# A decoder layer in split float32: the start addresses of the staged operands of the down projection and of the turned rows of the output projections

## The reference, cut to what matters

```python
h = rmsnorm(x, norm_attn_g);  proj = h @ w_in
mix = concat(differential_attention(...), stick_breaking_attention(...))
x = x + mix @ w_out                                              # 1024 x 1024
h2 = rmsnorm(x, norm_ffn_g)
x = x + (silu(h2 @ w_gate) * (h2 @ w_up)) @ w_down               # 1024 x 2816, 2816 x 1024
return rmsnorm(x, final_norm_g)
```

## Time and profile before

| | us |
|---|---|
| median of 3 runs (lowest, highest) | 2987.25 (2986.71, 2993.16) |
| profiled execution, its own time | 2989.48 |
| its span, first to last instruction | 2987.5 |
| PE busy | 2893.5 (97% of the span) |
| PEld busy | 2596.9 (87%) |
| DVE busy | 1961.6 (66%) |
| ACT busy | 1585.1 (53%) |
| mean granted TensorE clock | 0.994 of full |

### The profile page before, as it was taken

One profiled execution on the slowest core, in us unless ns is written; L12 is line 12 of the kernel. 1 busy time (PEld: TensorE's weight loads), 2 busy tenths in 40 slices (PEclk: granted clock), 3 DMA queues, 4 the chain that ended last, 5 costly groups with the idle time before them and its releaser, 6 DMA issues.

```text
span 2987.5 us, 51857 instructions
## 1 busy us (share of the span) xinstructions
PE 2893.5 (97%) x19000; PEld 2596.9 (87%) x19000; DVE 1961.6 (66%) x2944; ACT 1585.1 (53%) x2672; POOL 913.2 (31%) x1022
## 2 busy tenths in 40 slices
PE   7999999899999999999999999999999999999998
PEld 6888778677777999999889998998889998999886
DVE  6215520276776777778668787876658878888656
ACT  5122211267777878887555555554445555645444
POOL 1922221156665877777301222111000000001100
PEclk9999999999999999999999999999999999999999
DMA  5488896446642440411339998999747775799964
GB/s 202 127 213 210 200 244 155 127 103 145 162 112 60 112 99 16 114 32 62 113 124 285 321 310 261 286 278 310 211 134 218 237 238 184 218 325 295 293 195 159
DMA packets 303482, 559.47 MB, mean 187 GB/s; under 512 B 32289, under 2 KB 70305, under 8 KB 302113
## 3 DMA queue, kind: packets, MB, share of 16 engines
q1 hardware_dynamic: 262912, 463.12, 49.0%
q0 software_dynamic: 39072, 92.30, 16.2%
q10 hardware_dynamic: 1312, 1.64, 0.2%
HBM read 449.98 MB, written 197.13 MB: 217 GB/s over the span
## 4 chain that ended last, share of the span: by engine, by line
PE 59%; DVE 9%; POOL 6%; ACT 3%; issue 2%; DMA 2%; SPq 0%; DVEq 0%; ACTq 0%; POOLq 0%
PE f_ps L2431 26%; PE f_ps L2323 18%; PE h_o L998 6%; PE h_t L984 3%; PE h_z L720 2%; PE h_z L723 2%; POOL h_more L1282 2%; POOL h_work L1282 2%; DVE h_negmax L1118 2%; DVE h_more L1234 2%; DVE h_more L1150 1%; DMA f_wraw<-sums_scratch 1%; ACT h_work L1017 1%; ACT h_more L1017 1%; POOL h_srstd L1327 1%
## 5 line engine op out<-in xcount | busy, mean ns | idle before, releaser
L1810 ACT ACTIVATE f_whi<-f_wraw 128x512 fp32r<-128x512 f32 x834 | 520.4, 626 | 409.5 <-PE f_ps L2431 269.3
L1817 DVE TENSOR_TENSOR f_wlo<-f_wraw,f_whi 128x512 fp32r<-128x512 f32 x834 | 574.8, 690 | 237.9 <-ACT f_whi L1810 234.9
L2431 PE MATMUL f_ps<-f_hi_s,f_whi 128*128 128x256 f32 x1408 | 394.3, 280 | 6.1 <-DVE f_up L2164 6.0
L2431 PE MATMUL f_ps<-f_hi_s,f_wlo 128*128 128x256 f32 x1408 | 393.5, 279 | 0.0
L2431 PE MATMUL f_ps<-f_lo_s,f_whi 128*128 128x256 f32 x1408 | 392.5, 279 | 0.0
L1322 POOL TENSOR_TENSOR h_work<-h_work,h_more 128x1024 f32<-128x1024 f32 (+3 forms) x192 | 302.2, 1586 | 110.3 <-DVE h_more L1234 97.5
L2431 PE MATMUL f_ps<-f_hi_a,f_whi 128*128 128x256 f32 x1056 | 296.7, 281 | 0.9 <-DVE f_second L2164 0.9
L2431 PE MATMUL f_ps<-f_lo_a,f_whi 128*128 128x256 f32 x1056 | 296.6, 281 | 0.0
L2431 PE MATMUL f_ps<-f_hi_a,f_wlo 128*128 128x256 f32 x1056 | 295.5, 280 | 0.0
L2431 PEld LDWEIGHTS f_ps<-f_hi_s,f_whi 128*128 128x128 f32 x1408 | 265.1, 188 | 7.5 <-DVE f_wlo L1817 4.1
L2431 PEld LDWEIGHTS f_ps<-f_lo_s,f_whi 128*128 128x128 f32 x1408 | 264.7, 188 | 0.0
(11 more groups left out here) (199 smaller groups left out, 6857.1 us busy)
## 6 DMA issues: line engine op xcount, KB each, us to landing
f_wraw<-in_w_stream SPq DMA_DIRECT2D x394, 256.0 KB, 4.1
f_wraw<-sums_scratch SPq DMA_DIRECT2D x352, 256.0 KB, 4.5
sums_scratch<-in_w_stream POOLq DMA_DIRECT2D x132, 256.0 KB, 5.2
act_scratch<-f_act SPq DMA_DIRECT2D x88, 256.0 KB, 3.9
combined_acts<-f_act SPq DMA_DIRECT2D x88, 256.0 KB, 5.1
f_wraw<-down_sums SPq DMA_DIRECT2D x88, 256.0 KB, 2.7
f_piece<-combined_acts SPq DMA_DIRECT2D x88, 256.0 KB, 2.9
down_sums<-in_w_stream POOLq DMA_DIRECT2D x66, 256.0 KB, 6.5
```

The lines of the kernel that those rows point to most:

```text
L1810: act.activation(w_hi[ring][:], w_raw[ring][:], ACT.Copy).then_inc(S["hi_split"], 1)
L1817: dve.tensor_tensor(w_lo[ring][:], w_raw[ring][:], w_hi[ring][:].bitcast(F32), ALU.subtract).then_inc(S["lo_split"], 1)
L2431: mm = pe.matmul(outs[i], w[ring][:, col], a[name][:, c, :], start=(c == 0 and m == 0), stop=(c == 3 and m == 2))
```

## The change

`STAGE_SHIFT` places the three stages 96, 256 and 448 bytes behind a multiple of 512, hi and lo alike; turned pair 0 goes 128 bytes and pair 1 320 bytes behind it. The weights stay where they are. The buffers behind the stages (`pieces` and all that follow up to `junk`) move up by 512 bytes to make room. No instruction is added, removed or moved on any engine, and no size, wait or count changes.

```diff
+STAGE_SHIFT = (96, 256, 448)
...
-    pieces = stage + STAGES * row
+    pieces = stage + STAGES * row + LINE
...
-    assert junk + half <= H["base"] and stage + 2 * 4 * KC * BLK <= others
+    assert junk + half <= H["base"] and stage + 2 * 4 * KC * BLK + 320 <= others
...
-    F["turned_hi"] = [at(f"thi{n}", [P, KC, BLK], home, F32R) for n, home in enumerate((operands, stage))]
-    F["turned_lo"] = [at(f"tlo{n}", [P, KC, BLK], home + 4 * KC * BLK, F32R) for n, home in enumerate((operands, stage))]
+    F["turned_hi"] = [at(f"thi{n}", [P, KC, BLK], home, F32R) for n, home in enumerate((operands + 128, stage + 320))]
+    F["turned_lo"] = [at(f"tlo{n}", [P, KC, BLK], home + 4 * KC * BLK, F32R) for n, home in enumerate((operands + 128, stage + 320))]
...
-    F["stage_hi"] = [at(f"shi{s}", [P, BLK], stage + row * s, F32R) for s in range(STAGES)]
-    F["stage_lo"] = [at(f"slo{s}", [P, BLK], stage + row * s + half, F32R) for s in range(STAGES)]
+    F["stage_hi"] = [at(f"shi{s}", [P, BLK], stage + row * s + STAGE_SHIFT[s], F32R) for s in range(STAGES)]
+    F["stage_lo"] = [at(f"slo{s}", [P, BLK], stage + row * s + half + STAGE_SHIFT[s], F32R) for s in range(STAGES)]
```

## The result

| | before | after |
|---|---|---|
| median of 20 runs each, us | 2987.06 | 2995.47 |
| ratio, 95% interval | | 1.0027 (1.0016 to 1.0038) |
| profiled execution, its own time, us | 2989.48 | 2990.06 |
| its span, us | 2987.5 | 2988.0 |
| PE busy, us | 2893.5 | 2907.2 |

The change made the kernel slower by 0.27%, some 8 us. I had forecast 2981 us. The two profiled executions hide this, with spans 0.5 us apart: the attention in front of the changed part ended 10 us earlier in the one of after, and that differs from run to run. The first matmul of project and the end of the span tell more.

What follows compares the result with a forecast made beforehand. TensorE's own matmul pace was taken as the bound, PE busy 97%. Savings of 3.5 + 0.7 + 2.6 = 6.8 us, 0.9 on the path, gave 6.1 us: 2987.25 to 2981.1 us, range 2968 to 2992.

Steps and rivals of the forecast that it cites:

- the six that save 1.9 ns: Gate part, 256 columns: distances 32, 64, 128, 256, 288, 416 each save about 1.9 ns a matmul against 120 at 0.
- Stages: Down, 1848 matmuls at distances 416, 256 and 64: 1.9 ns saved on each, 3.5 us.
- Turned pair 0: Project blocks 0 and 3, 384 matmuls at distance 384: 1.9 ns saved on each, taken from neighbours 288 and 416, 0.7 us.
- Turned pair 1: Project blocks 1 and 2, 384 matmuls at distance 192: 6.7 ns saved on each, 2.6 us.
- 0.9 on the path: Project and down: 0.9 of TensorE's matmul time stands on the path; the rest is lost to waits on DVE or DMA.
- The two groups of three products: Gate tile: products at 32, 64, 128 took 117.8 ns a matmul, those at 256, 288, 416 took 118.3.
- The one on the bank: Gate part: s3 alone goes to the fourth bank of its four, which could cause its 113.3 ns instead of distance 192.
- Slower: All 2616 project and down matmuls: shifted weights meet the stream at a costlier moment, 8.5 us more, 2995.7 us; chance 0.14.
- What spoke for it: Attention scores: two 512 column matmuls at distance 0 took 230 ns each, so more than 13.4 ns can be lost.
- what spoke against it: Gate tile, 256 columns: neither half averages above the 120 ns of distance 0.
- No change: Project and down: the 13.4 ns are a fixed weight-change cost or the reads don't touch; 2987 us, chance 0.23.
- a large gain: Project and down: every distance does what 192 does in the gate part, 15.7 us less, 2971.5 us; chance 0.18.

Runs made afterwards that it cites:

- run with halves: Changed kernel with each project and down matmul, except the last two units, cut into two of 256 columns with own weight loads; 3001.29 us (before: 2984.41).
- sweep: Changed kernel with stages shifted by 32, 64, 160, turned pairs by 192, 224, gate operands by 192 to 512; 3005.19 us (before: 2985.87).
- 192 throughout: Kernel before with all seven gate operands 192 bytes behind a multiple of 512, nothing else changed; ratio 0.9964.

## Why the prediction was wrong

What I had asked about is there: the pace depends on the distance between the stationary slice and the moving operand. That it is the two reads which disturb each other fits this, but it is an inference; no run takes the weight load away. The step that failed is "distances 416, 256 and 64 are among the six that save 1.9 ns", with its like for pair 0 and pair 1: prices read at 256 columns were carried to 512.

- **Stages, -3.5 us forecast.** Measured: 624 matmuls at 234.0, 612 at 227.6 and 612 at 229.1 ns for 226.7, together 6.6 us more.
- **Turned pair 0, -0.7 us forecast.** 384 at 232.9 (233.4 in block 0, 232.4 in block 3): 2.4 us more.
- **Turned pair 1, -2.6 us forecast,** the largest single gain by matmul. 384 at 233.4: 2.6 us more. At 512 columns 192 is among the slow ones.
- **Sum.** 11.6 us more on TensorE, of which 0.9 on the path is 10.4 us; the median shows 8.4, the back part 10.9. From first matmul to first matmul the projects took 4.4 us more for 5.0 on TensorE, and the down stages from (0, 3) on 4.7 for 5.2, so the share of 0.9 was right there. That 10.9 is so near to 10.4 is in part luck: 3.4 of it come from down (0, 0 to 2), which differs by as much between runs with one and the same down part, and gates 1 and 3 gave 1.5 back.
- **The reading behind the prices.** The two groups of three products that I took for six distances at one price mix what differs. Distance 256 is among them, which by itself takes 120 (seven operands at 0) and saves nothing; 64, which had 117.5 there, had 113.4 in the run with halves. So "six of seven distances save 1.9" was no property of the distances even at 256 columns.
- **The doubts.** I had named two. The one on the bank was void (sweep, and 192 throughout). The other, that the load is as long as the matmul at 256 columns and covers half of it at 512, was the one that counted, and I priced it only on the side of a gain. The run with halves shows that the width decides. How the width turns the order round, no run shows; it stays open.
- **The rule of the Trainium skill,** in "TensorE: Matmul & The Clock Gate", section "Step-by-step: what each phase is for", that the next weight load takes no read bandwidth from the running matmul, is not borne out by the traces. By it no distance would matter, but the paces move by up to 7.3 ns of 226.7 and by 6.7 of 120.0 with nothing but addresses changed.
- **The rivals.** "Slower" named the place (all of L2323), the price (8.5 us, 2995.7 us) and the point of decision (229.2 ns; it is 230.2 in the long piece and 231.1 over all). Measured: 2995.47. I gave it 0.14. Its price had a slip: the earlier trace rows has 230 ns, which is 3.3 and not 3.6 above 226.7, so 7.8 us and 2995.0. The paces rose by 4.4 ns on average, so that the price came so close is in part luck. What spoke for it, had warned that 512 columns can lose more than 13.4 ns, though that row has distance 0, and no run explains it; what spoke against it came from 256 columns again. "No change" would have held for a shift of 256, "a large gain" for nothing.
- **What was costed at nothing.** ACT, DVE and the buffers moved by 512 cost nothing that can be told from noise, as the run with all at 256 shows (ratio 0.9989 to 1.0009). The gate part kept its pace.

## What to carry to other kernels

Where every matmul has a weight load of its own, the pace may hang on the difference of the start addresses of the two operands, here modulo 256 bytes. It can be read from start to start in a profile. Here it moved the pace by 1 to 3% at 512 columns and by up to 6% at 256 without an instruction changed. A price measured at one width of the moving operand must not be carried to another. And where a pace has two patterns, look at it stretch by stretch: a mean over the kernel hides that half of it runs in the slow one.

## What the runs showed of the hardware

- Float32r matmuls of project and down with a weight load each, granted clock 1.00 (2.4 GHz), start to start: 226.7 ns for 512 columns at a distance of 0 modulo 256 bytes, 229 to 234 ns at the other seven steps of 32 bytes. (In the attention has 230 ns.)
- 256 columns: 120.0 ns at 0, 113.3 or 117.8 at 192 (the one or the other for up to 1700 matmuls), 113.3 or 117.7 at 64, 117.5 to 119.0 elsewhere. Behind another distance up to the first eight matmuls take other times.
- 226.7 and 113.3 are the lowest paces that these matmuls held in any run. They are 17/16 of the time of the columns alone (213.3 and 106.7 ns). Whether less can be had wasn't tried.
